# Two weight rings with more slots, and small tiles laid out anew, in a kernel of two chained transformer blocks

## The reference, cut to what matters

```python
def expert_block(args):                       # first mixture, 32 experts
    xe, e = args
    gu = xe @ w_gate_up[e] + b_gate_up[e]     # 1024 x 2048
    gate = jnp.minimum(gu[:, :D_FF], SWIGLU_LIMIT)
    up = jnp.clip(gu[:, D_FF:], -SWIGLU_LIMIT, SWIGLU_LIMIT)
    act = (up + 1.0) * gate * jax.nn.sigmoid(SWIGLU_ALPHA * gate)
    return act @ w_down[e] + b_down[e]        # 1024 x 1024

def _swiglu(h, wg, wu, wd):                   # second mixture, 8 experts, width 1408
    return (jax.nn.silu(h @ wg) * (h @ wu)) @ wd
...
for e in range(N_EXPERTS_2):
    out = out + gates[:, e:e + 1] * _swiglu(hf, wg[e], wu[e], wd[e])
```

## Time and profile before

| | |
|---|---|
| median of 3 runs | 2715.33 us (2711.19 to 2717.74) |
| span of the profiled execution | 2714.8 us |
| TensorE busy | 2530.1 us, 93% |
| VectorE, ScalarE, GpSimd busy | 889.7, 541.9, 394.1 us |
| DMA | 734.14 MB, 270 GB/s on average |
| SP's queue | 712.02 MB, 66.2% of the 16 engines' span |

### The profile page before, as it was taken

The page is one execution under the profiler, slowest core; times in us unless marked ns, Lnnn a source line. Parts: engine busy times, 40 slices in busy tenths (PEclk is TensorE's granted clock), DMA queues, the critical chain, the costliest instruction groups (busy, mean ns, idle before and its releaser), DMA issues.

```text
span 2714.8 us, 38216 instructions
## 1 busy us (share of the span) xinstructions
PE 2530.1 (93%) x15435; PEld 1522.5 (56%) x15435; DVE 889.7 (33%) x1613; ACT 541.9 (20%) x1085; POOL 394.1 (15%) x527
## 2 busy tenths in 40 slices
PE   7999998999989899899898699998999999999996
PEld 4446667886433334334333268787887787844442
DVE  4667377023112111111211135551012446423223
ACT  2221244102212112121121131321001323300001
POOL 2000355301111111101111100221010011100010
PEclk9999999999999999999999889999999999999998
DMA  7334653549999999999999961127443211589997
GB/s 265 124 129 156 204 175 120 124 148 373 422 424 424 424 424 425 424 422 423 425 424 423 424 221 63 63 74 273 152 135 135 96 61 63 241 351 423 424 424 296
DMA packets 152854, 734.14 MB, mean 270 GB/s; under 512 B 12564, under 2 KB 41904, under 8 KB 107488
## 3 DMA queue, kind: packets, MB, share of 16 engines
q1 hardware_dynamic: 145008, 712.02, 66.2%
q0 software_dynamic: 7264, 19.45, 1.9%
q10 hardware_dynamic: 400, 0.15, 0.0%
HBM read 718.72 MB, written 12.85 MB: 269 GB/s over the span
## 4 chain that ended last, share of the span: by engine, by line
PE 75%; DMA 17%; DVE 4%; ACT 1%; issue 1%; POOL 1%; SPq 1%; DVEq 0%; ACTq 0%; POOLq 0%; PEldq 0%
PE P L863 73%; DMA R<-in_w_gate_up 10%; DVE R L1965 2%; PE P L866 2%; DMA WS<-in_w_gate_up 1%; DMA WS<-in_w_down 1%; DMA R<-in_moe_w_down 1%; DMA WS<-in_ffn_w_up 1%; ACT R L2916 1%; DMA R<-in_moe_w_up 1%; POOL R L3415 1%; DVE R L1971 1%; SPq L787 1%; DMA WS<-in_w_mod 0%; ACT L2916 0%
## 5 line engine op out<-in xcount | busy, mean ns | idle before, releaser
L863 PE MATMUL P<-R 128*32 128x256 f32 (+9 forms) x7452 | 993.6, 429 | 94.8 <-DMA R<-in_w_gate_up 48.1
L863 PEld LDWEIGHTS P<-R 128*64 128x64 f32 (+5 forms) x7452 | 502.5, 145 | 552.7 <-issue 435.2
L863 PE MATMUL P<-R,WS 128*128 128x256 f32 (+1 forms) x2160 | 571.8, 424 | 5.6 <-ACT R L2916 2.3
L2916 ACT ACTIVATE R<-P 128x256 f32<-128x256 f32 (+4 forms) x373 | 176.1, 478 | 1619.4 <-PE P L863 1327.6
L863 PEld LDWEIGHTS P<-R,WS 128*128 128x128 f32 x2160 | 406.7, 192 | 151.0 <-issue 104.1
L863 PE MATMUL P<-WS,R 128*32 128x256 f32 (+4 forms) x2848 | 411.7, 490 | 26.1 <-DMA WS<-in_w_gate_up 9.3
L863 PE MATMUL P<-xT,WS 128*128 128x256 f32 (+2 forms) x1728 | 399.7, 384 | 8.3 <-ACT xT L2916 3.5
L863 PEld LDWEIGHTS P<-xT,WS 128*128 128x128 f32 (+2 forms) x1728 | 317.3, 188 | 69.7 <-issue 17.7
L863 PEld LDWEIGHTS P<-WS,R 128*64 128x64 f32 (+2 forms) x2848 | 149.0, 127 | 244.6 <-issue 194.8
L1965 DVE TENSOR_TENSOR R<-P,R 128x512 f32<-128x512 f32 (+2 forms) x166 | 93.9, 578 | 505.4 <-PE P L863 456.0
L3531 POOL PARTITION_BROADCAST R<-R x180 | 122.8, 682 | 678.4 <-DVE R L1965 347.5
(11 more groups left out here) (246 smaller groups left out, 941.7 us busy)
## 6 DMA issues: line engine op xcount, KB each, us to landing
R<-in_w_gate_up SPq DMA_DIRECT2D x82, 2048.0 KB, 25.8
WS<-in_w_gate_up SPq DMA_DIRECT2D x46, 2048.0 KB, 31.9
R<-in_w_down SPq DMA_DIRECT2D x76, 1024.0 KB, 32.0
WS<-in_w_in SPq DMA_DIRECT2D x60, 1024.0 KB, 7.6
WS<-in_w_down SPq DMA_DIRECT2D x52, 1024.0 KB, 30.2
R<-in_moe_w_gate SPq DMA_DIRECT2D x22, 1408.0 KB, 14.8
R<-in_moe_w_up SPq DMA_DIRECT2D x18, 1408.0 KB, 17.4
WS<-in_w_mod SPq DMA_DIRECT2D x24, 1024.0 KB, 7.8
```

The lines of the kernel that those rows point to most:

```text
L863: return nc.tensor.matmul(out, lhsT, rhs, start=start, stop=stop, skip_group_check=True)
L2916: return nc.scalar.activation(out, in_, f, **kw)
```

## The change

RING becomes 18 and MRING 11. For that the first mixture's ring takes columns 0 to 24576 of R (12 slots), WS keeps six; what lay in R from 22528 on in that stage (XG, the two bias rows brows, iota1, wTt, Gw, Gx) moves. C1 and the small tiles cs32, wsel, ea and extra become views of one new tile T: C1 first, then T2 with 2048 columns. Slot 10 of the second mixture is 3072 columns of T from column 448 on, that is from the constant head to the 1920th column of T2; the few columns of extra that the second mixture needs (gsp, bsp, sum2, sums2, dk) move behind it. Its first loads go to the slots 4, 5, 10, 3, 0, 1, 6, 7, 8, 9, 2, so that load 2 is the first into the new slot and load 10 goes to slot 2. Later loads take the slots in the order of use, 11 turns back; those late in the mixture skip slots 0 and 1, which leaves them 10 and then 9 turns.

```diff
-RING = 16
+RING = 18
-MRING = 10
+MRING = 11
-MSLOT = [4, 5, 2, 3, 0, 1, 6, 7, 8, 9]
+MSLOT = [4, 5, 10, 3, 0, 1, 6, 7, 8, 9, 2]
+_given = iter(MTURN)
 for _n in range(MRING, 96):
-    MSLOT.append(MSLOT[MNTH[MTURN[_n - MRING + (2 if _n >= 90 else 0)]]])
+    _slot = MSLOT[MNTH[next(_given)]]
+    while _n > MNTH[7, "gate", 1] and _slot in (0, 1):
+        _slot = MSLOT[MNTH[next(_given)]]
+    MSLOT.append(_slot)
...
-        C1 = sb("C1", [128, a["const1"].shape[1]])
+        LATE = 448
+        first, wide1 = LATE - where1["head"][0], a["const1"].shape[1]
+        T = sb("T", [128, first + wide1 + 2048])
+        C1 = T[:, first:first + wide1]
+        T2 = T[:, first + wide1:]
-        cs32 = sb("cs32", [128, KT, 32])
+        cs32 = T2[:, 0:256].rearrange("p (k e) -> p k e", k=KT)
-        wsel = sb("wsel", [128, KT, NEXP])
+        wsel = T2[:, 256:512].rearrange("p (k e) -> p k e", k=KT)
-        extra = sb("extra", [128, 768])
+        extra = T2[:, 1280:2048]
-        ea = sb("ea", [128, 4, 192])
+        ea = T2[:, 512:1280].rearrange("p (c h) -> p c h", c=4)
...
-        XG = reg(23040, 2, KT, CAP)
-        brows = [reg(24064, 512), reg(22528, 512)]
+        XG = reg(26112, 2, KT, CAP)
+        brows = [T2[:, 512:1024], extra[:, 0:512]]
...
-        mring = [reg(2048 + 3072 * n, 3072) if n < 6 else ws[:, 3072 * (n - 6):3072 * (n - 5)] for n in range(MRING)]
+        mring = ([reg(2048 + 3072 * n, 3072) for n in range(6)] + [ws[:, 3072 * n:3072 * n + 3072] for n in range(4)]
+                 + [T[:, LATE:LATE + 3072]])
...
-            return WS[:, n - 10, :] if n >= 10 else reg(2048 * n, 2048)
+            return WS[:, n - 12, :] if n >= 12 else reg(2048 * n, 2048)
...
-                    if n == 2:
+                    if n == 3:
                         sp.wait_ge(S("mm_free"), START["out1"] + 4)
...
-                    if n in (10, 12, 14):
-                        sp.wait_ge(S("unit_used"), cu.n - 2 + (n - 10) // 2)
+                    if n in (12, 14, 16):
+                        sp.wait_ge(S("unit_used"), cu.n - 2 + (n - 12) // 2)
...
-                    if u % RING >= 10:
+                    if u % RING >= 12:
                         freed(*LOADS[u])
```

More of the change, by code:

```diff
@@ L342, in build @@
         CAP0 = 96
-        XG = reg(23040, 2, KT, CAP)
-        brows = [reg(24064, 512), reg(22528, 512)]
+        XG = reg(26112, 2, KT, CAP)
+        brows = [T2[:, 512:1024], extra[:, 0:512]]
         biasg = reg(25088, 512)
         biasu = reg(25600, 512)
[L347 to L350, removed]
+        iota1 = extra[:, 512:768]
+        wTt = T2[:, 1024:1280]
+        Gw = T2[:, 256:512].rearrange("p (c s) -> p c s", c=2)
+        Gx = [T2[:, 128 * i:128 * i + 128].rearrange("p (c s) -> p c s", c=2) for i in range(2)]
         gla = reg(27136, 512)
@@ L400, in build @@
         nK, q0, q1, rs, nm, nb = (st[:, at:at + 2] for at in (0, 2, 6, 10, 12, 4))
-        gsp, bsp, sum2, sums2 = extra[:, 0:8], extra[:, 8:16], extra[:, 16:32], extra[:, 48:64]
-        dk = extra[:, 40:42]
+        gsp, bsp, sum2, sums2 = extra[:, 704:712], extra[:, 712:720], extra[:, 720:736], extra[:, 752:768]
+        dk = extra[:, 744:746]
         grow1 = xT[:, 4:8, :].rearrange("p a b -> p (a b)")
@@ L575, in ring @@
         def ring(n):
-            return WS[:, n - 10, :] if n >= 10 else reg(2048 * n, 2048)
+            return WS[:, n - 12, :] if n >= 12 else reg(2048 * n, 2048)
         def ring_pair(n):
-            return WS[:, n - 10:n - 8, :].rearrange("p a b -> p (a b)") if n >= 10 else reg(2048 * n, 4096)
+            return WS[:, n - 12:n - 10, :].rearrange("p a b -> p (a b)") if n >= 12 else reg(2048 * n, 4096)
         def m_weights(e, kind, s):
@@ L710, in freed @@
                         sp.wait_ge(S(f"m_{kind}"), x + 1)
-                for n, (x, kind, s) in [(n, MLOADS[n]) for n in (0, 1, 4, 5, 2, 3, *range(6, len(MLOADS)))]:
+                for n, (x, kind, s) in [(n, MLOADS[n]) for n in (0, 1, 4, 5, *range(2, 4), *range(6, len(MLOADS)))]:
                     slot = MSLOT[n]
```

## The result

The changed kernel takes 2694.39 us (median of 6, 2692.30 to 2701.89), the kernel before beside it 2714.43 us (6 runs). The ratio is 0.9927, 95% interval 0.9917 to 0.9936: 20.0 us less, where 7.0 us were forecast. The profiled execution took 2693.65 us, its span is 2692.0 us.

A forecast was written before the change was run, and what follows sets the result against it. DMA was taken to bound both mixtures at 424 GB/s, so only pauses at their starts could be won: 3.6 + 3.4 = 7.0 us off 2715.33 gives 2708.3 us (chance 0.57), range 2702.6 to 2713.5.

The forecast's parts named there:

- Tiles laid next to each other: Small tiles become views of T and others move; instructions, sizes and waits stay the same: 0, bounds -1 to +1 us.
- The time is bytes divided by 424 GB/s.: In both mixtures' long stretches DMA engines never pause, so only a pause before such a stretch can be won.
- a fall under 420: Sign against the prediction: it is wrong if the DMA engines' rate falls under 420 GB/s.
- First mixture, 3.6 us: Ring of 18: two more down loads fill the pause, loads from 20 on come 3.6 us earlier; bounds 0 to 4.95.
- a pause of 1.9 us is new: First mixture: load 20 waits for quarter (0,3), released at 658.9, and reaches the engines at 659.8, leaving 1.9 us unused.
- Second mixture, 3.4 us: Ring of 11: load 10 is ordered without waiting, one load of 1408 KB ahead: 3.4 us gained, bounds 0 to 3.7.
- The end of the first mixture, 0: Layer 0's first units are ordered over 10 us earlier, worth nothing; bounds 0.3 us gained, 2.5 us lost.
- A: Rival: only the first mixture's gain arrives, as TensorE sets the second mixture's end; 2711.7 us, chance 0.12.
- B: Rival: a wait on SP ahead of loads 16 and 17, or 10, keeps new slots unfilled; 2715.3 us, chance 0.10.
- D: Rival: slower, both mixtures' tails run at half TensorE's clock, 13.5 us more; 2721.8 us, chance 0.07.
- C: Rival: no pause left in the first mixture (4.95), whole 1536 KB load counts in the second (3.7); 2706.6 us, chance 0.14.
- The rule that spoke against it: At the skill's 358 GB/s the first mixture's larger ring would be worth nothing, one load in the second 4.0 us.

The follow-up runs named there:

- a_rings_before: The changed kernel with both rings taken back to 16 and 10 slots, its layout as changed: 2702.48 us, ratio 0.9954 to the kernel before.
- b_al256: The kernel before with C1 laid out 224 bytes wider, so that R begins at a multiple of 256 bytes, rings as before: 2703.34 us, ratio 0.9965.

## Why the prediction was wrong

- **Tiles laid next to each other: 0, bounds -1 to +1.** This step failed. The layout is worth 12.5 us (a_rings_before), 10.9 by the 224 bytes alone (b_al256). Its reason was that no instruction, size or wait changes. That is true; but an address is an operand too, and the destinations of all loads into R had moved by 7392 bytes, from rest 32 to rest 0 by 256. It was the only line of the sum that touched every load of both mixtures, those into WS through the others (384 of 1024 KB, 64 of 1408, 24 of 1536 and 8 more of 1024 KB, 541 of the 734 MB), and it was costed by counting instructions.
- **"The time is bytes divided by 424 GB/s."** The same error, seen from the first step. The rate was read as a property of the chip because it was so even the earlier trace rows. Even it was; but all slices shared the same two tiles. The prediction did list the rate among its signs, with a fall under 420; it did not think of a rise.
- **First mixture, 3.6 us**: the mechanism was right, the size was somewhat low. SP's orders moved as forecast (3.4 us by the trace without this ring, 659.0 against 658.9), the pauses stand at 654 to 663, and the bias row ahead of the pair was not in its way. But the loads behind it came 4.7 to 5.1 us earlier by the landings, near the bound of 4.95. The term was "a pause of 1.9 us is new", with 0.5 us before it: from 35 to 75 us after the first order the engines leave 5.4 us unused in the kernel before and 5.7 to 6.5 in the three traces of the changed kernel with this ring taken back, and 1.4 to 1.7 in the three of the changed kernel, where 5.1 + 0.6 against 2.4 were reckoned. Timed it is 3.9 us.
- **Second mixture, 3.4 us**: right. 2.3 and 2.9 us timed, 2.8 to 4.5 us in the traces. The engines ran dry 44 us after the mixture's first order (2360 - 2316.16) where it had been 40 (2372.6 - 2332.27), and the wait for load 10 was gone.
- **The end of the first mixture, 0**: right. SP ordered the units of layer 0 at 1548.89, 14.2 us ahead of the last down's use on TensorE (1563.05), where it had been 0.5 us behind it, and the projection still waited for xT from VectorE (0.31 us). From the last down's group to the projection it took 10.2 us in place of 11.9. That is TensorE's clock, not the units: before, it was at 0.50 (1.2 GHz) in 1579, after at 1.00 (2.4 GHz) at the same point of the program (rows below), though TensorE had been as idle two microseconds earlier in both (0.18 and 0.22 busy), and two traces with the early units have 11.9 us again: the kernel with both tiles at 256, and the changed kernel itself run once more (after_again, 1560.63 to 1572.50).

The microsecond before (first row) and after (second row), columns as in the earlier trace rows:

```profile
1579.00:1580.00 1.00, 1.00 (x3) 0.80 (x3) 0.53 (x2) 0.98 (x3) 1.00 (x3) 0.50 1.05 399
```

```profile
1567.00:1568.00 1.00, 1.00 (x6) 0.88 (x5) 0.49 (x2) 0.94 (x3) 1.00 (x3) 1.00 1.06 398
```

- **The rivals.** A (only the first gain) and B (slots not filled) are out by the runs with one ring taken back. D (slower through the clock) is out: the tail's last group took 4.71 us, as before. C (8.7 us) isn't told from 7.0 by the times: the rings brought 6.2 (3.9 + 2.3) to 7.4 us with R at 256, and 8.5 and 10.8 us with R out of line. The landings (4.7 to 5.1 us) and the second mixture (3.5 us by the means of all traces with R at 256) make 8.2 to 8.6 us, nearer to C, though not by C's reason alone, for short pauses are left. No rival had a faster rate.
- **The rule that spoke against it**: the Trainium skill, SBUF — State Buffer, "Summary: rules for kernel authors", has about 358 GB/s for loads from HBM. The runs differ from it: with the queue full these loads ran at 421 to 430 GB/s in every kernel.

Place and rings measured apart, each by its own runs, are 10.9 (b_al256) to 12.5 us (a_rings_before) and 6.2 us; they make 17.1 to 18.7 us, against 20.0 measured. The ratios' intervals reach 2.4 us or more to either side, in each of the runs that this sum uses, so the 1.3 to 2.9 us left over can't be told from 0.

## What to carry to other kernels

Where DMA sets the time, write down the start of every tile that large loads go into, before and after a change, and see to it that each is a multiple of 256 bytes; small tiles of odd size belong behind the large ones or need a few unused columns. Any edit that adds, removes or reorders tiles may move them without a word in the diff. A rate that is the same in every slice is not yet a limit: ask what all those slices have in common.

## What the runs showed that was not expected

- The destination's start in SBUF is worth 1% of the rate for packets of 8 to 16 KB: 4 to 5 ns for each, be it 614, 423 or 310 ns long, and so 0.8% to 1.6%. With WS at rest 128, a rest of 32, 64 or 128 bytes for R costs nearly the same (618.9, 618.2 and 618.1 ns).
- It is not paid load by load. With six slots of sixteen out of line and ten in line the packets keep their shortest time (0.96), and with all in line nearly every one does (0.99). With R out of line the packets into the unmoved WS lose theirs too.
- The few groups of matmuls between the first mixture's last load and the next projection took 10.2 or 11.9 us in two traces of one kernel, with TensorE's clock at 1.00 or down to 0.50: a measure that ends behind such a tail carries that spread, one that ends at a landing doesn't.
- One core took 430 GB/s from HBM in some slices, with a DMA share of 1.01 both at this rate and at 424: the share does not tell a fast packet from a slow one.
